# Experts of a hybrid backbone step: gate and up products in steps of 512 columns, w_down in three passes

## The reference, cut to what matters

```
def swiglu(x, wg, wu, wd):
    return (jax.nn.silu(x @ wg) * (x @ wu)) @ wd

def moe(x, w_router_l, wg, wu, wd):
    logits = (x @ w_router_l).astype(jnp.float32)
    top_v, top_i = lax.top_k(logits, TOP_K)
    ...
    for e in range(N_EXPERTS):
        out = out + combine[..., e:e + 1] * swiglu(x, wg[e], wu[e], wd[e])
    return out
```

## Time and profile before

| what | us |
|---|---|
| median of 3 runs | 2135.04 (2134.25 to 2135.24) |
| the profiled execution, first to last instruction | 2131.6 |
| first gate/up product of the first expert | 1085.94 |
| last w_down product of the last expert | 2098.41 |
| TensorE busy | 1916.8 |
| VectorE busy | 909.3 |
| ScalarE busy | 675.0 |

### The profile page before, as it was taken

The page is one execution under the profiler, slowest core; times in us unless marked ns, Lnnn a source line. Parts: engine busy times, 40 slices in busy tenths (PEclk is TensorE's granted clock), DMA queues, the critical chain, the costliest instruction groups (busy, mean ns, idle before and its releaser), DMA issues.

```text
span 2131.6 us, 20882 instructions
## 1 busy us (share of the span) xinstructions
PE 1916.8 (90%) x7660; PEld 1289.0 (60%) x7661; DVE 909.3 (43%) x1352; ACT 675.0 (32%) x1026; POOL 109.5 (5%) x93
## 2 busy tenths in 40 slices
PE   6999898899996798999779898989999898999793
PEld 2444444788886796554656565656666566666562
DVE  0303602433335724442545555555555544333454
ACT  1103211433324222221234444444444443221342
POOL 2111110000000500000010000000000000000001
PEclk9999998999998897557679999999999999999897
DMA  9565659333334423001559999999999997544792
GB/s 298 188 214 182 198 203 358 121 119 119 99 119 93 125 80 99 1 1 59 178 173 303 324 325 314 333 315 313 307 326 301 322 299 261 178 148 159 235 297 110
DMA packets 359072, 436.78 MB, mean 205 GB/s; under 512 B 32332, under 2 KB 311528, under 8 KB 358968
## 3 DMA queue, kind: packets, MB, share of 16 engines
q1 hardware_dynamic: 334160, 397.44, 57.4%
q10 hardware_dynamic: 20456, 25.21, 3.4%
q0 software_dynamic: 4352, 12.88, 1.7%
HBM read 417.57 MB, written 17.93 MB: 204 GB/s over the span
## 4 chain that ended last, share of the span: by engine, by line
PE 81%; DVE 9%; issue 5%; ACTq 2%; ACT 2%; DMA 1%; DVEq 0%; POOL 0%; POOLq 0%
PE ps L1601 33%; PE ps L1618 15%; PE ps L1525 7%; PE ps L1566 5%; PE ps L1498 4%; PE ps L1629 4%; PE ps L1668 3%; PE ps L1731 3%; PE ps L1707 2%; DVE split L1219 2%; PE ps L1580 2%; PE ps L1680 2%; ACTq L821 2%; DVE ring_split L1283 1%; DVE extra_split L1283 1%
## 5 line engine op out<-in xcount | busy, mean ns | idle before, releaser
L1601 PE MATMUL ps<-split,hi_x 128*128 128x512 f32 (+1 forms) x2304 | 693.4, 386 | 25.0 <-issue 20.2
L1219 DVE TENSOR_TENSOR split<-ring,split 128x1024 fp32r<-128x1024 f32 (+1 forms) x432 | 469.1, 1131 | 103.3 <-ACT split L829 101.4
L1601 PEld LDWEIGHTS ps<-split,hi_x 128*128 128x128 f32 x2304 | 419.8, 193 | 110.6 <-issue 33.2
L1601 PE MATMUL ps<-split,lo_x 128*128 128x512 f32 (+1 forms) x1152 | 438.8, 381 | 0.0
L829 ACT ACTIVATE split<-ring 128x1024 fp32r<-128x1024 f32 (+1 forms) x432 | 389.3, 977 | 52.7 <-issue 35.2
L1618 PE MATMUL ps<-ring,work 128*128 128x512 f32 x792 | 357.9, 593 | 3.7 <-DVE work L1252 3.7
L857 ACT ACTIVATE work<-ps 128x256 f32<-128x256 f32 (+1 forms) x144 | 52.8, 367 | 691.8 <-PE ps L1601 691.7
L1246 DVE TENSOR_TENSOR work<-work,ps 128x256 f32<-128x256 f32 (+1 forms) x144 | 57.4, 399 | 479.1 <-ACT work L857 432.1
L1601 PEld LDWEIGHTS ps<-split,lo_x 128*128 128x128 f32 x1152 | 220.8, 192 | 42.1
L1618 PEld LDWEIGHTS ps<-ring,work 128*128 128x128 f32 x792 | 147.9, 189 | 150.6 <-issue 142.8
L1525 PE MATMUL ps<-ring,cond 128*2 128x256 f32 x576 | 128.0, 383 | 9.6 <-DMA ring<-in_w_mod_dram 9.6
(11 more groups left out here) (219 smaller groups left out, 1575.7 us busy)
## 6 DMA issues: line engine op xcount, KB each, us to landing
ring<-in_moe_w_gate_dram SPq DMA_DIRECT2D x80, 1024.0 KB, 7.4
ring<-in_moe_w_up_dram SPq DMA_DIRECT2D x80, 1024.0 KB, 9.9
ring<-in_moe_w_down_dram SPq DMA_DIRECT2D x80, 1024.0 KB, 5.1
ring<-in_w_mod_dram SPq DMA_DIRECT2D x36, 1024.0 KB, 7.4
mod_extra<-in_w_mod_dram SPq DMA_DIRECT2D x12, 1024.0 KB, 6.9
ring<-in_w_qkv_dram SPq DMA_DIRECT2D x6, 2048.0 KB, 8.9
ring<-in_w_in_dram SPq DMA_DIRECT2D x5, 2048.0 KB, 10.3
ring<-in_ffn_w_gate_dram SPq DMA_DIRECT2D x10, 1024.0 KB, 7.7
```

The source lines that it names most:

```text
L1219: dve.tensor_tensor(low, raw, high.bitcast(F32), ALU.subtract).then_inc(lo_ok, 1)
L1601: ins = pe.matmul(ps[:, 0, 0:2 * w], xt(c_), split[:, j % 2, part, c_, 0:2 * w], start=(c_ == 0 and n == 0), stop=(c_ == KC - 1 and n == 2))
```

## The change

Only the expert loop and what feeds it changes in substance; elsewhere semaphores are merged and renamed so that the new ones fit.

- The hidden columns go in six steps (`MW`), five of 512 and one of 256. Gate and up of a step are two products of 512 columns into two PSUM banks that share their token operand.
- Weights arrive in pieces: a step has four, each with two of the eight row blocks, as two DMAs of 0.5 MB with 2 KB runs. There are eight raw places, and the low part is written over the raw values. The high parts have only four places, one step (`G_HI`). A place of a high part is free when TensorE has used the piece (`gu_used`), and so is a raw place.
- w_down arrives in blocks of 128 rows (0.5 MB), six raw places; ScalarE and VectorE cut it into high and low parts, and TensorE takes three passes.
- The transposed hidden values are cut into high and low (`hidden_high` on ScalarE, `hidden_low` on VectorE) instead of copied.
- The next round's tokens are transposed in two halves through one PSUM bank, after the w_down products of steps 2 and 4.
- The final gain vector is loaded after the last round instead of during the routing.

```
+MW = [2 * SF] * 5 + [SF]
...
+G_RAW, G_HI = 8, 4
...
+D_RAW, D_HI = 6, 4
...
+            def rest_of_expert(e, gu_base, down_base):
+                todo = [("g", 2), ("g", 3), ("d", 0), ("g", 4), ("d", 1), ("g", 5), ("d", 2), ("d", 3)]
+                for kind, n in todo:
+                    for q in range(4):
+                        if kind == "g":
+                            p = G_PIECES * n + q
+                            gu_free(gu_base + (p - G_RAW + 1))
+                            gate_up_fill(e, p)
+                        else:
+                            f = D_RAW + 4 * n + q
+                            sp.wait_ge(down_used, STEPS - 1 + down_base + (f - D_RAW + 1))
+                            down_fill(e, f)
...
+                for p in range(G_RAW):
+                    gu_free(i * G_N + (p - G_RAW + 1))
+                    gate_up_fill(e, p)
+                for f in range(D_RAW):
...
+                rest_of_expert(e, i * G_N, i * D_N)
```

ScalarE's part (`gu_high` waits for `gu_used` and for the piece's DMA; the last step's pieces are the next expert's first):

```
+                def gu_high(j, pieces):
...
+                    for n in pieces:
+                        act.wait_ge(gu_used, i * G_N + (G_PIECES * j + n - G_HI + 1))
...
                 def moe_round(ks):
                     if 1 in ks:
...
+                        turned_in_second(i + 1)
+                    for j in range(MJ):
+                        if j:
+                            hidden_high(ks[-1], j - 1)
+                        if 1 in ks:
+                            moe_silu_out(0, j, 1)
+                            down_high_out(j, slice(0, 3))
+                            hidden_high(0, j)
+                            down_high_out(j, slice(3, 4))
+                        gu_high_ahead(j, range(3))
+                        moe_silu_out(ks[-1], j, ks[-1])
+                        if j == MJ - 1:
+                            turned_in_half(0, i * 2 + 3)
+                        gu_high_ahead(j, (3,))
+                        if 1 not in ks:
+                            down_high_out(j, slice(0, 4))
+                    turned_in_half(1, i * 2 + 4)
+                    hidden_high(ks[-1], MJ - 1)
```

VectorE's part has the same order with the low parts (`hidden_low`, `gu_low_ahead`, `moe_hidden`, `turned_in_half`, `down_low_out`), and ends with the copy of the result. Two subtractions behind `moe_hidden` are `turned_in_half(0)` and piece 3 of the next step. TensorE's part:

```
+                        for kk in range(2):
+                            c_ = 2 * n + kk
+                            for m, (tokens, part) in enumerate(((xg_hi, g_high), (xg_lo, g_high), (xg_hi, g_low))):
...
+                                    for g in range(2):
+                                        ins = pe.matmul(ps[:, g, :], tokens[k][:, c_, :], both[:, g, kk, :],
+                                                        start=start, stop=stop)
...
+                        for m, (part, wt) in enumerate(((0, d_high), (1, d_high), (0, d_low))):
+                            for hf in range(2):
+                                ins = pe.matmul(ps[:, 3 + 2 * k + hf, :], h_split[:, part, q, :],
...
                     for u in range(len(todo) + 1):
                         if u:
                             pj_, pk = todo[u - 1]
...
+                            expert_turn(pj_, pk)
                         if u < len(todo):
                             j, k = todo[u]
...
+                            expert_gate_up(j, k, k == 0, k == ks[-1])
                         if u:
...
+                            expert_down(pj_, pk, ks)
+                        if u == len(todo) - 3:
+                            turn_half(0, i * 16 + 32, i * 2 + 2)
+                        if u == len(todo) - 1:
+                            turn_half(1, None, i * 2 + 3)
```

More of the change, by code:

```diff
@@ L49 @@
 EXPERTS = 8
+MW = [2 * SF] * 5 + [SF]
+MS = [sum(MW[:j]) for j in range(len(MW))]
+MJ = len(MW)
+G_PIECES = 4
+G_N = MJ * G_PIECES
+G_RAW, G_HI = 8, 4
+D_N = D_FF // P
+D_RAW, D_HI = 6, 4
+D_FILLS = [sum(f % D_RAW == s for f in range(D_N)) for s in range(D_RAW)]
 EPS = 1e-6
@@ L539, in _ @@
+            rest_of_expert(0, 0, 0)
             sp.wait_ge(route_ok, 1)
@@ new lines, in gu_high_ahead, with down_high_out @@
+                def gu_high_ahead(j, pieces):
+                    if j + 1 < MJ:
+                        gu_high(j + 1, pieces)
+                    else:
+                        with act.If(left > 1):
+                            gu_high(MJ, pieces)
+                def down_high_out(j, part):
+                    for f in step_down(j)[part]:
+                        act.wait_ge(d_full[f % D_RAW], i * (16 * D_FILLS[f % D_RAW]) + 16 * (f // D_RAW + 1))
+                        if f >= D_HI:
+                            act.wait_ge(down_used, STEPS - 1 + i * D_N + (f - D_HI + 1))
+                        act.activation(d_high(f), d_raw(f), ACT.Copy).then_inc(down_hi, 1)
@@ L1440, in _, with gu_low_ahead @@
                 left = dve.snap(rounds - i, min_val=1, max_val=2 * EXPERTS)
-                def split_ahead(j, of_round, pieces):
-                    split_low(j, slot_of(F_MOE + j), of_round * (PIECES * STEPS) + PIECES * (STEPS + j), pieces)
+                def gu_low_ahead(j, pieces):
+                    if j + 1 < MJ:
+                        for n in pieces:
+                            p = G_PIECES * (j + 1) + n
+                            gate_up_low(p, i * G_N + (B_W + p + 1))
+                    else:
+                        with dve.If(left > 1):
+                            for n in pieces:
+                                gate_up_low(n, i * G_N + (B_W + G_N + n + 1))
@@ new lines, in moe_round @@
+                        turned_in_second(i + 1)
+                    for j in range(MJ):
+                        if j:
+                            hidden_low(ks[-1], j - 1)
+                        if 1 in ks:
+                            moe_hidden(0, j)
+                            down_low_out(j, slice(0, 3))
+                            hidden_low(0, j)
+                            down_low_out(j, slice(3, 4))
+                        gu_low_ahead(j, range(3))
+                        moe_hidden(ks[-1], j)
+                        if j == MJ - 1:
+                            turned_in_half(0, i * 2 + 3)
+                        gu_low_ahead(j, (3,))
+                        if 1 not in ks:
+                            down_low_out(j, slice(0, 4))
@@ L1790, in moe_round @@
+                    todo = [(j, k) for j in range(MJ) for k in ks]
                     for u in range(len(todo) + 1):
```

482 lines of the change are left out of this document (268 added, 214 removed).

## The result

The changed kernel takes 2225.16 us (median of 4 runs, 2222.76 to 2230.39), the kernel before 2134.64 in the runs beside it: a ratio of 1.043, with a 95% interval of 1.041 to 1.045. The forecast was 2125 us, with 2090 to 2155 as its range: wrong in sign, and 100 us off. The profiled execution spans 2223.7 us, the sum had said 2121.8.

The account below looks back on a forecast made before the run. TensorE was taken to bound the expert loop. Five single rounds +4.5, first +5.8, two-tile -14.6 and last -5.5 gave -9.8: span 2131.6 to 2121.8, plus 3.4 for the median, 2125 us, range 2090 to 2155.

Parts of the forecast that it names:

- Removed and added on TensorE: Mid-round on TensorE: w_down in three passes, 2.77 us against 3.43 per 256 rows; a full step takes 17.07 us.
- cuts on ScalarE and VectorE: Mid-round: pieces cost VectorE 2.25 us and ScalarE 1.9, w_down blocks 1.16 and 1.05; both engines stay below 17.07 per step.
- Start of a round: From E, the end of the old round's last w_down product: TensorE waits 6.1 us after the first product, before 7.93.
- End of a round: From B, the start of the last, half-width product: single-tile round ends at B + 27.0, near B + 14.5 without waits.
- the landing: At a round's end, the third piece of the next expert's weights arrives by DMA at B + 11.4, uncertain by 1.5 us.
- the two waits: TensorE waits twice, about 5 us each, in the last 17 us of a round, ended by VectorE.
- the first round: First round of the expert loop: 112.3 us against 106.5, so +5.8.
- Two tiles: Round with two token tiles: 198.8 us against 213.4, so -14.6, with a tail free of late DMA.
- Last round: Last round of the expert loop, with no next pieces to load: 114.5 us against 120.0, so -5.5.
- Shorter gap: VectorE's 9.20 us gap at round starts vanishes: -4.1 a round; 2097 to 2100 us; chance 0.25, shared with earlier landing.
- TensorE fetches anew: At each branch back TensorE fetches its loop body again, 13.15 us each: 2184 us; chance 0.08.
- DMA bound: DMA queues bound each round if they run below 349 GB/s: 2151 us at 335, 2180 at 320; chance 0.15.

Follow-up runs that it names:

- the mended one: Changed kernel with both new SyncE orders, next expert's pieces behind the last hidden values, fewer ScalarE waits, result copied between pieces two and three: 2080.5 us, ratio 0.973.

## Why the prediction was wrong

**Removed and added on TensorE; cuts on ScalarE and VectorE.** Right. 17.15 us a step against 17.07; pieces 2.29 and 1.91 against 2.25 and 1.9, blocks 1.22 and 1.05 against 1.16 and 1.05. TensorE set the pace in mid-round.

**Start of a round: the step that failed**, E + 26.2 in place of E + 17.8, some 42 us over five rounds. The step reads "VectorE copies the result, branches back, 9.20, and is there at E + 9.9". It carried a gap over from the old trace as if it belonged to the engine, and gave ScalarE, which had none, a cost of nothing, though every addition of the change to that engine's loop (new pieces, blocks, waits, in two bodies) stood in the diff. The gap belongs to a loop at a place: it left VectorE, whose loop shrank, and came to ScalarE twice, once behind each of its two branches. There it costs time, since ScalarE now stands first in the chain of the first step. With ScalarE's loop moved the second product begins 14.2 us after E (1201.46 to 1215.67): earlier than the 17.8 forecast, for the 9.20 is gone too and ScalarE cuts pieces under TensorE's first product. Two errors of opposite sign, +12.0 and -3.6. The second product itself takes 12.62 us behind the long wait (granted clock 0.86) and 11.12 with the loop moved (1.00), so that a round falls by 13.6 in all.

**End of a round.** The mechanism was right: SyncE's pause (14.5 us between the issues at 1277.90 and 1292.37; forecast 12.9), ScalarE behind the landing, the two waits. What was mis-sized is the landing: the third piece is cut from 1310.46, B + 13.9, not B + 11.4. The pieces are not issued "all at once" with the end of the w_down product at B - 0.4 but from 1297.64, B + 1.1, behind four blocks, and then follow each other by 2.7 to 2.8 us. SyncE's issues, and ScalarE at the third piece:

```profile
1277.90 1.42 SPq L576 DMA_DIRECT2D ring<-in_moe_w_down_dram  x2
1292.37 4.51 SPq L576 DMA_DIRECT2D work<-in_moe_w_down_dram  x4
1297.64 0.38 SPq L572 DMA_DIRECT2D ring<-in_moe_w_gate_dram  x1
```

```profile
1310.46 1.91 ACT L1003 ACTIVATE split<-ring 128x2048 fp32r<-128x2048 f32 x1 [0.80 <-DMA ring<-in_moe_w_up_dram]
```

That is the +2.45, 12 us in five rounds, and it stands in the first round's +2.2 too.

**Two tiles: the second step that failed**, 245.0 in place of 198.8. It said "a tail without late DMA" and took the rest from the count of matmuls. SyncE's order had been followed for a round with one tile only. With two, the second tile's gate/up product, which frees the pieces, lies behind the w_down product that frees the blocks, and the blocks queue behind the pieces: three steps of about 31 us in place of 17.1, 41.4 us. The run with the order turned gives 203.6, 4.8 above the forecast; where these stand was not worked out.

**Last round** 114.2 for 114.5: right in the sum only. With ScalarE's loop moved it is 109.6, so ScalarE's gap stood in this round too, and the other terms had been set too high.

**Rivals.** *Shorter gap*: the condition came true, VectorE's gap did vanish, and what it would have paid is seen in the kernel before with VectorE's loop moved: 6 us a round (114.5 to 108.5). *TensorE fetches anew*: right mechanism, wrong engine. *DMA bound*: not in the changed kernel (288 GB/s over five rounds); near in the mended one (344 to 346 at a share of 0.95), below the 349 that the rival had put as its point, at rounds of 104 to 109 us.

The Trainium skill (Runtime: NRT & Kernel Launch, Instruction fetch mechanics), which the prediction cited for VectorE and TensorE, says further that an engine other than TensorE holds two blocks of 256 instructions. The runs agree with two blocks: a loop from 654 to 1004 stays held, one from 630 to 906 doesn't. That size alone could have been set against the loop that the diff builds for ScalarE.

**What stays open.** Where the edges of the blocks lie was worked out from which loops had gaps, not read anywhere, and no run measured that a block is 256 instructions. The mended kernel still shows 25 instruction packets in the stretch of the 27 above, with no gap on ScalarE. They are SyncE's: the run that gave only SyncE a second body, for two tiles, shows 50 there, and the one that only reordered SyncE's loop 30. The first of these:

```profile
q14 instruction: 50, 0.41, 0.2%
```

## What to carry to other kernels

Before a change adds code to a loop with a branch back, count the instructions of that loop on every engine, not only on the one that shows a gap now, and treat a gap with no releaser as a property of where the loop lies: some satisfied waits ahead of it, executed once, can take it away (2225 to 2157 us here, 2134 to 2105 in the old kernel) or bring it (2080 to 2133). Follow the order of each DMA queue through every shape of the loop body, as an order that fits one shape can put the transfer needed next behind one that can't start. When one engine is moved to the head of a chain, cost its absence and not only its work.

## What the runs showed of the hardware

- One fetch behind a branch held ScalarE 5.2 to 6.4 us, and 6.2 to 6.9 where one gap was left; two fell on every start of a round with one tile in the changed kernel. The packets on the instruction queue are 8 KB each (0.22 MB in 27). The Trainium skill (Runtime: NRT & Kernel Launch, Instruction fetch mechanics) speaks of blocks of 16 KiB; no run here shows whether two packets make one.
- Six instructions more ahead of an unchanged loop cost 52 us (2080.5 to 2132.8), and 24 more ahead of another won 68.
- In the changed kernel ScalarE loads its function table twice in the first step of a round with one tile (1.28 us at the first copy, 1.28 at Silu), and not between Silu and the copies behind it.
